# A delta-rule scan: sixteen-row blocks of its inverses solved on VectorE instead of three doubling levels on TensorE

## The reference, cut to what matters

```
a_mat = where(strict, beta * (k k^T) * decay, 0)
sol   = triangular_solve(eye + a_mat, [beta * v, beta * exp(g) * k], lower, unit_diagonal)
u, w  = split(sol)
v_new = u - w S ;  o = (q exp(g)) S + attn v_new ;  S = S exp(g_last) + k_dec^T v_new
```

## Time and profile before

| what | us |
|---|---|
| median of three runs | 9719.1 |
| the profiled execution | 9733.38 |
| its span, first to last instruction | 9731.6 |
| TensorE busy | 7168.3 |
| VectorE busy | 5011.9 |
| GpSimd busy | 3808.6 |
| ScalarE busy | 1743.6 |

### The profile page before, as it was taken

How to read it: one execution, slowest core, us unless ns; L and a number is a source line. 1 busy time by engine, 2 the same in 40 slices (tenths; PEclk the granted TensorE clock), 3 DMA queues, 4 the chain that set the end, 5 groups by cost and what they waited for, 6 DMA issues and landing times. The chain is left out here.

```text
span 9731.6 us, 86153 instructions
## 1 busy us (share of the span) xinstructions
PE 7168.3 (74%) x32042; PEld 4736.7 (49%) x32042; DVE 5011.9 (52%) x7685; ACT 1743.6 (18%) x3270; POOL 3808.6 (39%) x2854
## 2 busy tenths in 40 slices
PE   5989568799761677777669885687987617777676
PEld 2877458799341222222238764587983402222222
DVE  3322757432547666665433226564325475666654
ACT  0012234222100111111100122342222001111111
POOL 0310512100213777777613104121002147777776
PEclk8989779888885999999989897798888859999999
DMA  4322430100425999999943224201014169999999
GB/s 167 117 97 84 164 130 36 44 32 20 177 74 195 368 380 379 380 374 407 358 165 114 95 96 173 102 36 44 32 45 161 71 221 367 372 378 378 369 398 360
DMA packets 637344, 1936.00 MB, mean 199 GB/s; under 512 B 70997, under 2 KB 142037, under 8 KB 632409
## 3 DMA queue, kind: packets, MB, share of 16 engines
q0 software_dynamic: 368640, 1342.34, 36.1%
q1 hardware_dynamic: 268298, 588.32, 16.8%
HBM read 1794.55 MB, written 142.19 MB: 199 GB/s over the span
## 5 line engine op out<-in xcount | busy, mean ns | idle before, releaser
L621 PE MATMUL expert_acc<-expert_row,expert_diag 128*128 128x512 f32 x4864 | 2404.8, 622 | 1181.7 <-DMA expert_row<-in_peer_v,expert_idx 769.6
L739 DVE CUSTOM_DVE_ANT_0 expert_junk<-expert_row,expert_h 128x1024 f32<-128x1024 f32 x1280 | 1560.5, 1226 | 1233.3 <-DMA expert_row<-in_peer_u,expert_idx 1196.2
L621 PEld LDWEIGHTS expert_acc<-expert_row,expert_diag 128*128 128x128 f32 x4864 | 852.3, 193 | 2729.1 <-issue 1388.0
L588 POOL DMA_INDIRECT expert_row<-in_peer_u,expert_idx x1280 | 1421.7, 1111 | 661.7 <-issue 389.6
L588 POOL DMA_INDIRECT expert_row<-in_peer_v,expert_idx x1280 | 1387.4, 1084 | 390.3 <-issue 275.6
L655 ACT ACTIVATE expert_diag<-expert_ident,expert_wt 128x128 f32<-128x128 f32 x1216 | 472.7, 399 | 2381.6 <-PE expert_acc L621 2303.1
L337 POOL TENSOR_TENSOR proj_wl<-proj_w,proj_wh 128x4096 fp32r<-128x4096 f32 (+1 forms) x40 | 354.8, 8870 | 1351.3 <-DVE proj_wh L385 1351.3
L1089 PE MATMUL mcols_ps<-mcols_w,hidden_hT 128*128 128x256 f32 x2560 | 619.3, 397 | 124.6 <-ACT mcols_o L1098 103.6
L314 PE MATMUL proj_ps<-proj_wl,proj_hT 128*128 128x512 f32 (+1 forms) x1600 | 629.7, 394 | 97.3 <-POOL proj_wl L337 97.3
L314 PE MATMUL proj_ps<-proj_wh,proj_hT 128*128 128x512 f32 (+1 forms) x1600 | 629.1, 393 | 0.0
L314 PE MATMUL proj_ps<-proj_wh,proj_hTl 128*128 128x512 f32 (+1 forms) x1600 | 628.6, 393 | 0.0
(11 more groups left out here) (453 smaller groups left out, 10836.2 us busy)
## 6 DMA issues: line engine op xcount, KB each, us to landing
proj_w<-in_w_in SPq DMA_DIRECT2D x30, 2048.0 KB, 9.8
mod_w<-in_w_mod SPq DMA_DIRECT2D x24, 2048.0 KB, 7.7
mcols_w<-in_w_in SPq DMA_DIRECT2D x32, 1024.0 KB, 6.7
scratch_PR<-proj_o SPq DMA_DIRECT2D x30, 1024.0 KB, 5.3
rprep_xs<-scratch_PR SPq DMA_DIRECT2D x30, 928.0 KB, 12.7
gprep_xs<-scratch_PR SPq DMA_DIRECT2D x30, 768.0 KB, 8.5
scratch_RQ<-rprep_res SPq DMA_DIRECT2D x10, 2304.0 KB, 7.9
rw_x<-scratch_RQ SPq DMA_DIRECT2D x40, 512.0 KB, 6.9
```

The lines of the kernel that those rows point to most:

```text
L588: pool.indirect_dma_start(out=slot(kind, n), out_offset=None, in_=e.peer_u if kind == "dot" else e.peer_v, in_offset=bass.IndirectOffsetOn ...
L621: mm = pe.matmul(acc[:, i % 2, c, :], diag[:, done % DIAGS, :], slot("sum", n)[:, c * CHUNK:(c + 1) * CHUNK], start=(k == 0), stop=(k == P ...
L739: dve.tensor_tensor_reduce(junk[:, n % 2], slot("dot", n), h[:, i % 2], 1.0, 0.0, ALU.mult, ALU.add, hid[:, k:k + 1]).then_inc(s.dot, 1)
```

## The change: a base solve on VectorE

Blocks of sixteen rows on the diagonal are inverted in another way, by forward substitution, one block per partition: 8 matrices times 8 blocks make 64 blocks, on 64 partitions. Of the six doubling levels the first three go; the three for blocks of 16, 32 and 64 stay (`HIGH = 3`).

To bring a block into one partition's row and the result back, SP makes an exchange through DRAM in each unit: eight transfers of `a`'s diagonal blocks out (`NG`, pieces of 64 bytes), two in (`low`, `got`), one of the results out (`XG`), and four back (`small`, pieces of 64 bytes), each step waiting for the one before. VectorE solves between them: fifteen times a product and a sum over the last axis, each waiting for the one before, and a transposed copy. Then it spreads the results under a block mask into `invT` and `inv`. The turns are ordered anew, so that HGRN's first levels and a gate turn stand where the exchange runs.

```
+BASE_LEVELS = 4
+BASE = 1 << BASE_LEVELS
+BLOCKS = P // BASE
...
-SCAN_TURNS = "gh" * 3 + "ghghz" * 6 + "gh"
+SCAN_TURNS = "gh" * 3 + "hzhg" + "hzhhg" + "ghz" * 4 + "gh" * 3 + "h"
...
+        HIGH = LEVELS - BASE_LEVELS
+        G_LANES = P // 2
+        lanes_of = lambda d: slice(d * G_LANES // 2, (d + 1) * G_LANES // 2)
...  (SyncE)
+                def exchange(u):
+                    sp.wait_ge(s.A, 2 * u + 1)
+                    for b in range(BLOCKS):
+                        here = slice(b * BASE, (b + 1) * BASE)
+                        sp.dma_start(e.NG.rearrange("(n b) (i j) -> b i n j", b=BLOCKS, i=BASE)[b],
+                                     a[here, :, here]).then_inc(s.nb, 16)
+                    sp.wait_ge(s.nb, 16 * BLOCKS * (u + 1))
+                    for d, dst in enumerate((low, got)):
+                        sp.dma_start(dst[lanes_of(d)].rearrange("p i j -> p (i j)"), e.NG[lanes_of(d), :])\
+                          .then_inc(s.lane, 16)
+                    sp.wait_ge(s.binv, u + 1)
+                    sp.dma_start(e.XG.rearrange("w p c -> p w c"),
+                                 base_inv[0:G_LANES].rearrange("p w i j -> p w (i j)")).then_inc(s.xb, 16)
+                    sp.wait_ge(s.xb, 16 * (u + 1))
+                    for d in range(2):
+                        for k in range(2):
+                            sp.dma_start(small[:, k, 4 * d:4 * d + 4, :],
+                                         e.XG[k ^ d, lanes_of(d), :].rearrange("(n b) (i j) -> (b i) n j", n=4, i=BASE))\
+                              .then_inc(s.small, 16)
...
+                ld(eye[:].rearrange("p i j -> p (i j)"), e.eye_base)
+                ld(blocks[:].rearrange("p b j -> p (b j)"), e.base_blocks)
...
+                    exchange(u)
                     sp.wait_ge(s.oc, 2 * (u + 1))
...  (TensorE; ScalarE's levels change in the same way)
-                    for d in range(2):
-                        pe.wait_ge(sd[d].x, 6 * u + 1)
-                        turn_round(d, inv)
...
+                    yield
+                    yield
-                    for v in range(1, LEVELS):
+                    for q in range(HIGH):
+                        v = BASE_LEVELS + q
...
-                            if v > 1:
+                            if q:
                                 turn_round(d, invT)
...  (VectorE)
-                    for d in range(2):
-                        step(dve.tensor_copy(of_dir(inv, d), over4(ident[:])))
-                    dve.wait_ge(s.A, 2 * u + 1)
-                    for d in range(2):
-                        dve.copy_predicated(of_dir(inv, d), over4(below[:, 0, 1 - d, :]), of_dir(a, d))\
-                           .then_inc(sd[d].x, 1)
...
+                    by_row, flipped = base_inv[0:G_LANES, 0], base_inv[0:G_LANES, 1]
+                    mine = slice(0, G_LANES)
+                    dve.wait_ge(s.lane, 32 * (u + 1))
+                    step(dve.tensor_copy(low[lanes_of(1)], got[lanes_of(1)].rearrange("p i j -> p j i")))
+                    step(dve.tensor_copy(by_row, eye[mine]))
+                    for r in range(1, BASE):
+                        step(dve.tensor_tensor(prod[mine, 0:r, 0:r],
+                                               low[mine, r, 0:r].unsqueeze(1).to_broadcast([G_LANES, r, r]),
+                                               by_row[:, 0:r, 0:r].rearrange("p j c -> p c j"), ALU.mult))
+                        step(dve.tensor_reduce(by_row[:, r, 0:r], prod[mine, 0:r, 0:r], AX.X, ALU.add))
+                    dve.tensor_copy(flipped, by_row.rearrange("p i j -> p j i")).then_inc(s.binv, 1)
+                    yield
+                    dve.wait_ge(s.small, 64 * (u + 1))
+                    for k in (1, 0):
+                        for d in range(2):
+                            dst, done = ((inv, sd[d].x), (invT, sd[d].xt))[k]
+                            wide4 = [P, 4, BLOCKS, BASE]
+                            dve.tensor_tensor(of_dir(dst, d).rearrange("p n (b j) -> p n b j", b=BLOCKS),
+                                              small[:, k, 4 * d:4 * d + 4, :].unsqueeze(2).to_broadcast(wide4),
+                                              blocks[:].unsqueeze(1).to_broadcast(wide4), ALU.mult).then_inc(done, 1)
+                    yield
-                    for v in range(1, LEVELS):
+                    for q in range(HIGH):
+                        v = BASE_LEVELS + q
```

More of the change, by code:

```diff
@@ L1564, in scan_stage @@
         w = st.sb("w", [P, 2, 4, 64])
+        eye, blocks = st.sb("eye", [P, BASE, BASE]), st.sb("blocks", [P, BLOCKS, BASE])
+        got, low, prod = (st.sb(n, [P, BASE, BASE]) for n in ("got", "low", "prod"))
+        base_inv, small = st.sb("baseinv", [P, 2, BASE, BASE]), st.sb("small", [P, 2, 8, BASE])
         ula, res, vnew, kdec, go = ediff, ediff, dec, decT, erow
@@ L1577, in scan_stage @@
         s = named(**{n: st.sem("g" + n) for n in
-                     "t tc gsum ula G gcopy kk E1 E2 er D gl egl A DT ks res vn vnc o oc kdec st fin".split()})
+                     "t tc gsum ula G gcopy kk E1 E2 er D gl egl A DT ks res vn vnc o oc kdec st fin nb lane binv xb small".split()})
         sd = [named(**{n: st.sem(f"g{n}{d}") for n in "x xt T W wc D".split()}) for d in range(2)]
@@ L1712, in gdn @@
                         for d in range(2):
-                            pe.wait_ge(sd[d].wc, 6 * u + v)
-                            pe.wait_ge(sd[d].x, 6 * u + v)
+                            pe.wait_ge(sd[d].wc, HIGH * u + q + 1)
+                            pe.wait_ge(sd[d].x, HIGH * u + q + 1)
                             for n in range(4):
@@ L1811, in hgrn @@
                     yield
-                pe.wait_ge(s_const, 16 * 10)
+                pe.wait_ge(s_const, 16 * 12)
                 scan_turns(gdn, hgrn, lambda u: iter(()))
@@ L1833, in gdn @@
                     yield
-                    for d in range(2):
-                        act.wait_ge(sd[d].T, 6 * u + 1)
-                        act.copy(of_dir(invT, d), bank(YB + d)).then_inc(sd[d].xt, 1)
                     yield
-                    for v in range(1, LEVELS):
+                    yield
+                    yield
+                    for q in range(HIGH):
                         for d in range(2):
-                            act.wait_ge(sd[d].W, 6 * u + v)
+                            act.wait_ge(sd[d].W, HIGH * u + q + 1)
                             act.copy(w[:, d].rearrange("p n c -> p (n c)"), ps[:, XB + d, 0:256]).then_inc(sd[d].wc, 1)
-                            if v > 1:
-                                act.wait_ge(sd[d].T, 6 * u + v)
+                            if q:
+                                act.wait_ge(sd[d].T, (HIGH - 1) * u + q)
                                 act.copy(of_dir(inv, d), bank(YB + d)).then_inc(sd[d].x, 1)
@@ L1921, in gdn @@
                     t.then_inc(s.kdec, 1)
-                    for _ in range(2 * (LEVELS - 1) + 1):
+                    for _ in range(2 * HIGH + 3):
                         yield
@@ L1991, in gdn @@
                     yield
-                    for v in range(1, LEVELS):
+                    by_row, flipped = base_inv[0:G_LANES, 0], base_inv[0:G_LANES, 1]
[9 more added lines that the diff above has]
+                    dve.tensor_copy(flipped, by_row.rearrange("p i j -> p j i")).then_inc(s.binv, 1)
+                    yield
+                    dve.wait_ge(s.small, 64 * (u + 1))
[6 more added lines that the diff above has]
+                                              blocks[:].unsqueeze(1).to_broadcast(wide4), ALU.mult).then_inc(done, 1)
+                    yield
+                    for q in range(HIGH):
+                        v = BASE_LEVELS + q
                         yield
                         for d in range(2):
-                            dve.wait_ge(sd[d].D, 6 * u + v)
-                            dve.wait_ge(sd[d].xt, 7 * u + v)
+                            dve.wait_ge(sd[d].D, HIGH * u + q + 1)
+                            dve.wait_ge(sd[d].xt, (HIGH + 1) * u + q + 1)
                             change = ps[:, XB + d, 256:512].rearrange("p (n a b) -> p n a b", n=4, b=1 << v)
@@ L2081, in hgrn @@
                     yield
-                dve.wait_ge(s_const, 16 * 10)
+                dve.wait_ge(s_const, 16 * 12)
                 scan_turns(gdn, hgrn, gates)
@@ L2719, in constants @@
         "iota16": np.tile(np.arange(TOPK, dtype=np.float32), (P, 1)),
+        "eye_base": np.tile(np.eye(BASE, dtype=np.float32).reshape(1, BASE * BASE), (P, 1)),
+        "base_blocks": (j // BASE == t // BASE).astype(np.float32),
     }
@@ L2754 @@
     "RQ": (CTX + LAT, 9 * RW), "QH": (CTX + LAT, 2048),
+    "NG": (P // 2, BASE * BASE), "XG": (2, P // 2, BASE * BASE),
 }
```

7 lines of the change are left out of this document (3 added, 4 removed).

## The result

The changed kernel takes 9836.4 us, the median of four runs (9823.5 to 9841.7), the kernel before, run beside it, 9727.2 (9714.6 to 9739.9). The ratio is 1.0113, with a 95% interval of 1.0095 to 1.0131: slower by about 109 us. The forecast was 9841, which is +122 on the 9719.1 that it started from; as times the two lie 5 us apart, as changes 13, because the kernel before came out 8 us higher beside it. The profiled execution has a span of 9839.7 us.

A forecast was written before the change was run, and what follows sets the result against it. TensorE was taken as the bound in the doubling levels, waiting for VectorE in the front. Unit terms summed to 107.6 us against 95.6, +120 for ten; with 2 for constants, 9855 profiled, less 14.3 for the median: 9841 us, range 9775 to 9895.

The forecast's parts named there:

- `a` and the way out: Unit's start: `a` ready at 17.5 us, blocks exchanged by about 35 us, before VectorE comes to them, so no term.
- VectorE's way to the solve: VectorE before the solve: first `queries` end at about 33.0 us, GpSimd's instructions hold others, solve starts at 41.0.
- The solve: Fifteen products and sums plus copies on VectorE: 9.5 us, plus 3.0 waiting for GpSimd's keys, ending at 53.5.
- The way back: Results through DRAM to the spread: 6.8 us, to 60.3; W begins at 61.0 after a TensorE gap of some 15.
- Slow pieces: Rival on the transfers back: 64-byte pieces make them take 11.9 us, unit 112.7, total 9892 us; chance 15%.
- From W on: TensorE from first W to unit's end: 22.9 + 16.05 + 1.84 + 2.0 + 2.3 + 1.5 us.
- The lower clock: TensorE just after the gap ahead of W: running at the 1.2 GHz level was charged 2.3 us per unit.
- The wait of the last product: Unit's end: HGRN's last product on TensorE waits for VectorE's `queries` and collect behind GDN's state, 2.0 us.
- late masked writes: First kept level: its masked write stands behind other VectorE work; 1.5 us allowed, between 0 and 4.
- Ten times the unit: Both scan stages: each of ten units grows by 12.0 us, from 95.6 to 107.6, so 120 us in all.
- the gap that closes: Rival ahead of W: no GpSimd holds, W begins at 50.9 us, unit 93.7, total 9702 us; chance 4%.
- Short holds: Rival before the solve: GpSimd holds VectorE less, W begins at 56.5 us, unit about 103, total 9795; chance 20%.

The follow-up runs named there:

- e5: The changed kernel with its turns in another order, GDN's four front turns and the solve first: 9698.8 us, 0.9957 of the kernel before.
- e7: The changed kernel with GpSimd's fourth keys waiting for the end of the solve: 9816.7 us, a ratio of 1.0095 to the kernel before.
- e8: The changed kernel with 62 extra 128x128 products on TensorE in the gap ahead of the first W, results unused: 9824.4 us, ratio 1.0095 to before.
- e1: The changed kernel without the solve's fifteen product-and-sum steps, transfers, copies and spread kept: 9737.3 us, a ratio of 1.002 to the kernel before.
- e9: The changed kernel as it is, run once more: 9835.3 us, a ratio of 1.0103 to the kernel before.
- e4: The changed kernel with fifty extra 128x128 products on TensorE in the gap ahead of the first W, results unused: 9840.3 us, ratio 1.0113 to before.

## Why the prediction was right, step by step

- **`a` and the way out.** Ready 17.5 us into the unit, as forecast, and the transfers were no term.
- **VectorE's way to the solve.** The first queries end at 32.7 (33.0 forecast), the solve starts at 40.2 (41.0). The gate instruction L2065 behind them took 2.84 us beside GpSimd's second keys, and the second queries 2.06 beside its `kdec`.
- **The solve.** 12.7 us against 12.5. Undisturbed it is 9.96 (e5), against 9.5: a sum's element costs (0.38 - 0.146) / 225 = 1.04 ns as assumed, but a product's (0.53 - 0.15) / 224 = 1.7 ns (0.15 is the product of one element), where 1.03 was taken. The waiting for keys is 2.75 us against 3.0: 1.44 in place of 0.37 in the first copy and 2.12 in place of 0.39 to 0.44 in one product; e7 shows the second to be of the keys; for the copy it is argued, from e5, where no keys lie beside it. The long product ended 0.25 us after the keys did. The product of 121 elements, which had begun 0.21 us ahead of those keys, took 0.35 us, and the sum just behind it, which lay wholly beside them, 0.27, both as in e5 (0.36 and 0.27). This is what the Trainium skill ("SBUF — State Buffer", section "Who interferes with whom") states, and the trace agrees.
- **The way back.** 6.1 us (6.8), W at 59.9 (61.0), the gap 14.15 (15). Slow pieces did not come: `small`, in pieces of 64 bytes, landed 1.8 to 2.4 us after its issue. The Trainium skill's preference for 512 bytes or more ("DMA: Bandwidth & Descriptors", section "Specifications") is not contradicted, only not felt at this size: the store of `a`'s blocks in such pieces landed in 1.4 to 1.7.
- **From W on.** 49.4 us against 46.6: here a term was mis-sized. The lower clock was put at 2.3 us, where L1682 had lost 1.8; it lasts through HGRN's product into D and costs 4.1 in this unit, 3.3 on average (e8). The wait of the last product was 2.09 (2.0), but behind it stands a second stretch at the lower clock, 3.48 us for a product of 1.95, which the sum did not have. The 1.5 us allowed for late masked writes (L2047) were hardly needed, as TensorE waits only 3.1 us for them in all ten units, and nearly made up for it.
- **Ten times the unit.** In the first layer the four units that were summed grew by 13.2 us, not 12.0, in the second by 10.0. The sum took one unit of the first layer for all ten, but the second layer's units of before were 98.9 us long and not 95.6 (below). The two errors went against each other, and the stages' +115.1 lies close to the 120 by luck as well as by the sum. The 2 us for two constants ahead of each stage can't be told from a scatter of 10 us there.

Of the rivals, the gap that closes needed W before 52.8 us; it came at 59.9, and even without the solve at all (e1) the kernel is not faster than before. Short holds needed 56.5; slow pieces an 11.9 us way back.

## What to carry to other kernels

Work taken off the bound engine is worth its time only if the engine has other work while the replacement runs: here 12.9 us went by the sum, and in its place stood a gap of 14 us, 8.5 us of smaller waits and a clock that was slow to come back. Look first at where the replacement's latency lies in the order of turns: the kernel with the exchange is 1.1% slower than before in one order and 0.4% faster in another. The old algorithm in another order gains 0.6%, so that gain speaks for the order and not for the exchange. Price small edits from the stretch they are in, since a whole program's scatter hides them.

## What the runs showed of the hardware

After the same wait the lower clock can come in one pass of a loop and not in another. The timeline of TensorE of the kernel before, at the same place of a unit in the first layer and in the second:

```profile
1676.63 1.97 PE L1716 MATMUL scan_ps<-scan_w,scan_inv 128*128 128x64 f32 x16 [1.87 <-ACT scan_inv L1844]
1678.44 2.00 PE L1785 MATMUL scan_ps<-scan_ql,scan_kl 128*128 128x128 f32 x16
...
6427.52 3.29 PE L1716 MATMUL scan_ps<-scan_w,scan_inv 128*128 128x64 f32 x16 [1.89 <-ACT scan_inv L1844]
6430.61 3.73 PE L1785 MATMUL scan_ps<-scan_ql,scan_kl 128*128 128x128 f32 x16
```

After a wait of 1.87 us the one goes on at a granted clock of 1.00, the 2.4 GHz level; after 1.89 us the other, at 0.53 over the two products, needs nearly twice as long. The units behind the first of the second layer are 3.3 us longer for it (98.9 against 95.6), with the same instructions. In the changed kernel, too, such units differ by more than a microsecond (108.2 to 109.6, and 107.2 to 109.6 in e9), though W begins 59.6 to 60.3 us into each. In the experiments with a filled gap, W or the product behind it ran at the lower clock after waits of 2.8 us and more (e4), and neither did after waits of 0.2 to 1.6 us (e8). So what a wait costs beyond itself differs from pass to pass, and what decides it is not shown here.
